# Token norms of a two-layer transformer kernel: root and reciprocal with the tokens on the partitions

## The reference

```python
def rms_norm(t, g):
    tf = t.astype(jnp.float32)
    y = tf * lax.rsqrt(jnp.mean(tf * tf, axis=-1, keepdims=True) + EPS)
    return y.astype(t.dtype) * g

def modulate_2(t, g, shift, scale):
    return rms_norm(t, g) * (1 + scale) + shift
```

## The kernel before

| norm | place | tokens | turn on TensorE behind the sums | first product |
|---|---|---|---|---|
| 1 | before feed-forward 1 | 256 | none | L318 |
| 2 | before the mixer | 256 | `after`, 32 records | L318 |
| 3 | before feed-forward 2 | 256 | none | L318 |
| 4 | before MLA | 512 | `late`, 32 records | L1758 |
| 5 | before PEER, layer 0 | 512 | `after`, 32 records | L318 |
| 6 | before the differential attention | 512 | `late`, 64 records | L1675 |
| 7 | before PEER, layer 1 | 256 | none | L318 |

## Time and profile before

### The profile page before, as it was taken

The page is one execution under the profiler, slowest core; times in us unless marked ns, Lnnn a source line. Parts: engine busy times, 40 slices in busy tenths (PEclk is TensorE's granted clock), DMA queues, the critical chain, the costliest instruction groups (busy, mean ns, idle before and its releaser), DMA issues.

```text
span 3421.4 us, 53779 instructions
## 1 busy us (share of the span) xinstructions
PE 3250.2 (95%) x20550; PEld 2969.2 (87%) x20550; DVE 2388.9 (70%) x3963; ACT 1430.3 (42%) x1692; POOL 1060.6 (31%) x670
## 2 busy tenths in 40 slices
PE   7999889998999999899989999999988999999998
PEld 5999689755877999898989999997778999988787
DVE  6877577685753689987749989986664965026665
ACT  5435244323533333365523333324334468434443
POOL 0110000010000477776754335540001976740000
PEclk9999799999999999999999999999999999999999
DMA  8884157451022377799999999983114669768885
GB/s 317 333 293 167 50 193 251 159 192 55 1 75 89 117 270 257 250 361 362 383 353 394 379 386 406 409 337 111 38 59 157 230 211 306 258 232 289 298 286 206
DMA packets 305190, 814.27 MB, mean 238 GB/s; under 512 B 21760, under 2 KB 188928, under 8 KB 253696
## 3 DMA queue, kind: packets, MB, share of 16 engines
q1 hardware_dynamic: 241856, 583.07, 47.7%
q0 software_dynamic: 58752, 213.94, 16.7%
q10 hardware_dynamic: 4416, 15.05, 1.1%
HBM read 722.84 MB, written 89.13 MB: 237 GB/s over the span
## 4 chain that ended last, share of the span: by engine, by line
PE 72%; DVE 10%; DMA 3%; ACT 2%; issue 1%; SPq 1%; POOL 0%; DVEq 0%; ACTq 0%; POOLq 0%
PE ps L2735 19%; PE ps L3048 14%; PE ps L3040 10%; PE ps L1675 5%; PE ps L861 3%; PE ps L2297 3%; PE ps L1420 2%; PE ps L2757 2%; PE ps L318 2%; PE ps L872 2%; PE ps L1403 2%; PE ps L2137 1%; DVE arena L2773 1%; DMA arena<-activations 1%; DVE arena L2517 1%
## 5 line engine op out<-in xcount | busy, mean ns | idle before, releaser
L2735 PE MATMUL ps<-xT_split,arena_split 128*128 128x384 f32 (+1 forms) x4096 | 915.6, 312 | 15.0 <-POOL arena_split L2708 8.3
L2708 POOL TENSOR_TENSOR arena_split<-ring,arena_split 128x1024 fp32r<-128x1024 f32 x256 | 631.9, 2479 | 932.6 <-ACT arena_split L2662 931.5
L2735 PEld LDWEIGHTS ps<-xT_split,arena_split 128*128 128x128 f32 x4096 | 697.0, 191 | 16.3 <-issue 13.6
L2735 PE MATMUL ps<-hT_split,arena_split 128*128 128x384 f32 (+1 forms) x2048 | 634.8, 310 | 0.0
L3048 PE MATMUL ps<-arena_split 128*128 128x384 f32 x3072 | 535.4, 335 | 13.3 <-DVE arena_split L3000 13.3
L3048 PEld LDWEIGHTS ps<-arena_split 128*128 128x128 f32 x3072 | 534.2, 188 | 14.5 <-issue 12.3
L285 DVE TENSOR_TENSOR arena_split<-ring,arena_split 128x2048 fp32r<-128x2048 f32 x128 | 292.9, 2292 | 246.8 <-ACT arena_split L279 245.9
L2973 ACT ACTIVATE arena_split<-ring 128x2048 fp32r<-128x2048 f32 x128 | 245.5, 1918 | 482.6 <-PE ps L3048 287.7
L279 ACT ACTIVATE arena_split<-ring 128x2048 fp32r<-128x2048 f32 x128 | 244.4, 1915 | 378.5 <-PE ps L861 133.3
L2735 PEld LDWEIGHTS ps<-hT_split,arena_split 128*128 128x128 f32 x2048 | 391.9, 191 | 0.0
L2997 DVE TENSOR_TENSOR arena_split<-ring,arena_split 128x2048 fp32r<-128x2048 f32 x128 | 293.1, 2290 | 102.6 <-ACT arena_split L2973 102.6
(11 more groups left out here) (319 smaller groups left out, 5117.7 us busy)
## 6 DMA issues: line engine op xcount, KB each, us to landing
ring<-in_weights SPq DMA_DIRECT2D x396, 1024.0 KB, 5.2
arena<-in_side_weights POOLq DMA_DIRECT2D x152, 512.0 KB, 5.6
gates<-arena SPq DMA_DIRECT2D x48, 512.0 KB, 11.6
arena<-gates SPq DMA_DIRECT2D x32, 768.0 KB, 12.5
arena<-activations SPq DMA_DIRECT2D x64, 384.0 KB, 10.6
activations<-arena SPq DMA_DIRECT2D x128, 128.0 KB, 3.0
gates<-arena SPq DMA_DIRECT2D x16, 1024.0 KB, 7.8
arena<-gates SPq DMA_DIRECT2D x64, 256.0 KB, 5.1
```

Source lines behind the costliest of these rows:

```text
L2708: pool.tensor_tensor(low, self.raw(f)[:, j, :], high.bitcast(F32), ALU.subtract)\
L2735: mm = pe.matmul(k.ps[:, j, 0:self.T], self.u[:, 2 * (f % 2) + j, a, t * P:(t + 1) * P], self.h[b][:, t, :], start=n == 0, stop=n == 3 * D ...
```

## The change

A class `TokenRoots` takes the place of the sums, root and reciprocal of `Norm`:

- `table` runs a root of one column on ScalarE ahead of the squares.
- `add` takes 128 tokens of a squared tile as the stationary operand and one column of ones as the moving one, so the sum lands with tokens on the partitions, one column for each 128 tokens.
- `roots` and `invert` work on 2 or 4 columns; `invert` then scales the identity by each column.
- `along_tokens` multiplies ones by each scaled identity, which writes the reciprocal of every token along the free axis on all partitions, into bank 5. The scaling of the tiles reads it there, in PSUM.
- TensorE's order is now: sums, turn `late`, `along_tokens`, turn `after`.

```diff
+class TokenRoots:
+    def __init__(self, k, T, bank):
+        self.k, self.T, self.n = k, T, T // P
+        self.bank = bank
+        self.root, self.inv = k.root[:, 0:self.n], k.root[:, 8:8 + self.n]
+        self.diag = k.rstd[:, 0:T].rearrange("p (q n) -> p q n", n=P)
+        self.rstd = k.ps[:, bank, 0:T]
...
+    def table(self, act):
+        act.wait_ge(self.k.ones_ready.sem, self.k.ones_ready.at(1))
+        act.activation(self.k.small[:, 400:401], self.k.eps[:, 0:1], ACT.Sqrt)
+
+    def add(self, pe, t, sq):
+        for q in range(self.n):
+            mm = pe.matmul(self.k.ps[:, 0, q:q + 1], sq[:, q * P:(q + 1) * P], self.k.ones[:, 0:1],
+                           start=t == 0 and q == 0, stop=t == DT - 1, skip_group_check=True)
+        if t == DT - 1:
+            mm.then_inc(self.sums.sem, 1)
+
+    def roots(self, act):
+        act.wait_ge(self.sums.sem, self.sums.at(1))
+        act.activation(self.root, self.k.ps[:, 0, 0:self.n], ACT.Sqrt, bias=self.k.eps[:, 0:1],
+                       scale=1.0 / D).then_inc(self.rooted.sem, 1)
+
+    def invert(self, dve):
+        dve.wait_ge(self.rooted.sem, self.rooted.at(1))
+        dve.reciprocal(self.inv, self.root).then_inc(self.inverse.sem, 1)
+        dve.wait_ge(self.inverse.sem, self.inverse.at(1))
+        for q in range(self.n):
+            dve.tensor_scalar(self.diag[:, q, :], self.k.ident, self.inv[:, q:q + 1], None, ALU.mult)\
+               .then_inc(self.placed.sem, 1)
+
+    def along_tokens(self, pe):
+        for q in range(self.n):
+            pe.wait_ge(self.placed.sem, self.placed.at(q + 1))
+            mm = pe.matmul(self.k.ps[:, self.bank, q * P:(q + 1) * P], self.k.ones[:], self.diag[:, q, :],
+                           start=True, stop=True)
+        mm.then_inc(self.spread.sem, 1)
+
+    def wait_spread(self, dve):
+        dve.wait_ge(self.spread.sem, self.spread.at(1))
...
     def scalar(self, act):
         k, w = self.k, slice(self.lo, self.hi)
+        self.roots.table(act)
         for t in range(DT):
...
-        mean_root(k, act, self.sums, self.hi - self.lo, D, self.root)
+        self.roots.roots(act)
...
             pe.wait_ge(self.squares.sem, self.squares.at(t + 1))
-            mm = pe.matmul(k.ps[:, 0, 0:self.hi - self.lo], k.ones[:], self.sq[:, t, w], start=t == 0, stop=t == DT - 1)
-        mm.then_inc(self.sums.sem, 1)
-        for turn in (self.late, self.after):
-            if turn:
-                turn.tensor(pe)
+            self.roots.add(pe, t, self.sq[:, t, w])
+        if self.late:
+            self.late.tensor(pe)
+        self.roots.along_tokens(pe)
+        if self.after:
+            self.after.tensor(pe)
...
-        dve.wait_ge(self.root.sem, self.root.at(1))
-        dve.reciprocal(k.rstd[:, 0:T], k.root[:, 0:T]).then_inc(self.inverse.sem, 1)
-        dve.wait_ge(self.inverse.sem, self.inverse.at(1))
+        self.roots.invert(dve)
         if self.late:
             self.late.vector(dve)
+        self.roots.wait_spread(dve)
...
                 dve.scalar_tensor_tensor(k.hT[:, t, lo:hi], k.xT[:, t, lo:hi], gain[:, t:t + 1],
-                                         k.rstd[:, lo - self.lo:hi - self.lo], ALU.mult, ALU.mult)\
+                                         self.roots.rstd[:, lo - self.lo:hi - self.lo], ALU.mult, ALU.mult)\
                    .then_inc(self.scaled.sem, 1)
```

More of the change, by code:

```diff
@@ L656, in mean_root @@
                    scale=1.0 / width).then_inc(root_ready.sem, 1)
+class TokenRoots:
[5 more added lines that the diff above has]
+        self.rstd = k.ps[:, bank, 0:T]
+        self.sums = k.count_of("norm_sums", 1)
+        self.rooted = k.count_of("norm_root", 1)
+        self.inverse = k.count_of("norm_inverse", 1)
+        self.placed = k.count_of("norm_diag", self.n)
+        self.spread = k.count_of("norm_spread", 1)
+    def table(self, act):
[26 more added lines that the diff above has]
+        dve.wait_ge(self.spread.sem, self.spread.at(1))
 class Norm(Stage):
@@ L673, in __init__ @@
         self.squares = k.count_of("norm_squares", DT)
-        self.sums = k.count_of("norm_sums", 1)
-        self.root = k.count_of("norm_root", 1)
-        self.inverse = k.count_of("norm_inverse", 1)
+        self.roots = TokenRoots(k, self.hi - self.lo, 5)
         self.scaled = k.count_of("norm_scaled", DT * len(parts))
```

## The result

The changed kernel takes 3438.4 us (median), the kernel before in the same series 3421.9. The ratio is 1.005, 95% interval [1.0039, 1.0062]: slower, by 16.5 us, where the forecast was +9.6; the time lies 0.6 us inside the upper end of the forecast's range. The profiled execution has a span of 3438.3 us and a time of its own of 3440.1, so 1.8 us lie around the span; the forecast added its sum to a span as if nothing did.

The account below looks back on a forecast made before the run. TensorE, busy 95% of the span, was taken as the bound, each norm costing a wait plus products at the lower clock. Shifts 1.2 + 1.8 - 0.2 + 3.1 + 0.4 + 3.8 - 0.5 = +9.6 on 3421.4 gave 3431.0 us, range 3412 to 3439.

Parts of the forecast that it names:

- Rival (a): Narrow sums: one-column products count as work for the clock, which stays up; sum -7.6, 3413.8 us; chance 0.27.
- Rival (d): Narrow sums: the clock falls, but a one-column record keeps 0.11 us; +0.6, 3422.0 us; chance 0.03.
- Rival (c): Root in seven norms: the early table does not last, each pays up to 1.28 us; 3440 us; chance 0.05.
- norms 1, 3, 4 and 5: Forecast shifts of the work that follows each norm: +1.2, -0.2, +3.1 and +0.4 us.
- TensorE wins back 1.5 where it waited for a split chunk (L977): Norm 2: of 3.3 us lost to the turn `after`, 1.5 regained at that wait, leaving +1.8 us.
- norms 2 and 6: Forecast shifts of the work that follows these norms: +1.8 and +3.8 us.
- a fall at 3.8 us and a rise 4.4 us behind the turn's start: Norm 6: clock drops 3.8 us into the narrow sums, returns 4.4 us into the turn `late`.
- 0.7 is won back at a split chunk: Norm 6, behind the first product: 0.7 us of the delay regained, leaving +3.8 us.
- my lower end of 2.3: Narrow sums: earliest clock fall assumed, 2.3 us after their start, from a one-column stretch.
- the middle of two rows, 3.8 us: Narrow sums: clock fall taken between 2.3 us (one-column stretch) and 5.3 us (L1764's stretch).
- Norm 7: Forecast -0.5 us: full clock in the sums, which end as it falls; the rest shrinks from 2.3 to 1.8.

Follow-up runs that it names:

- e1: The changed kernel with the sums moving 128 columns of ones instead of one; 3415.6 us, ratio 0.9987 against the kernel before.
- e8: The changed kernel run once more, nothing altered, for a second trace; ratio 1.0045 against the kernel before.
- e4: The changed kernel with the new form only in the norms of 512 tokens (4, 5, 6), the old form elsewhere; ratio 1.003 against the kernel before.
- e6: The changed kernel with the turn `after` put ahead of the spreading (`along_tokens`) again; ratio 1.0065 against the kernel before.

## Why the prediction was right and wrong

**Right: the mechanism and the sign.** Clock 1.00 at the start of the narrow sums and 0.50 later, in norms 4, 5 and 6, with 0.11 and then 0.21 us a record. Rival (a), that the clock stays, falls by norm 5's window above; what it said would follow is what e1 measured, where the clock did stay: -1.9 and -5.4 us for norms 4 and 5 there, -1.5 and -5.0 here. Rival (d), a load that keeps its pace, falls too: L682's records, as far apart with one column (0.11 us) as e1's with 128, double in distance when the clock falls. The Trainium skill (TensorE: Matmul & The Clock Gate, section LDWEIGHTS) gives a load's time as its columns over 1.2 GHz, with no word of the clock, which makes an estimate of 107 ns for 128 columns. At clock 1.00 the trace agrees, with 0.11 us a record; at 0.50 it does not, with 0.21. Rival (c) falls: the table load stands ahead of the squares and no other comes before the root.

**Right within 0.5 us: norms 1, 3, 4 and 5.** Norm 1's scaling starts at 47.19 (forecast 47.2), and the reason is the forecast one: the load at 35.14 pushes the low halves. They move by 1.1 us, not 1.5, and what follows them takes 0.4 us longer than forecast, two small misses that cancel. The timelines of ScalarE and VectorE in norm 1, the answer to the earlier trace rows:

```profile
35.14 1.28 ACT L677 ACT_TABLE_LOAD   x1 [0.72 <-issue]
36.44 0.20 ACT L677 ACTIVATE small<-eps 128x1 f32<-128x1 f32 x1
36.55 2.54 ACT L744 ACTIVATE hT<-xT 128x256 f32<-128x256 f32 x8
```

```profile
40.99 4.49 DVE L285 TENSOR_TENSOR arena_split<-ring,arena_split 128x2048 fp32r<-128x2048 f32 x2 [4.97 <-ACT arena_split L279]
45.40 0.15 DVE L696 RECIPROCAL root<-root 128x2 f32<-128x2 f32 x1
45.59 0.48 DVE L699 TENSOR_SCALAR rstd<-rows,root 128x128 f32<-128x128 f32 x2
47.19 0.87 DVE L800 SCALAR_TENSOR_TENSOR hT<-xT,coef,ps 128x256 f32<-128x256 f32 x2 [1.12 <-PE ps L706]
```

In norm 4 (TensorE's timeline, the answer to the earlier trace rows) the narrow sums take 10.4 us (forecast 10.1), the turn 5.3 (5.6), and the clock is back before the first product:

```profile
658.31 10.50 PE L682 MATMUL ps<-ones,arena 128*128 128x1 f32 x64 [0.75 <-ACT arena L744]
668.67 5.50 PE L630 MATMUL ps<-ones,hT 128*128 128x128 f32 x32
674.01 1.06 PE L706 MATMUL ps<-rstd,ones 128*128 128x128 f32 x8
676.74 1.55 PE L1812 MATMUL ps<-hT,ring 128*128 128x512 f32 x3 [1.67 <-ACT hT L758]
```

In norm 5 the shift is right partly by luck. The sums took 11.4 us (forecast 10.1), so that scaling starts 1.9 us later counted from the start of the sums (forecast 0.6); but the clock came back early in the turn, which took 4.4 us instead of the forecast 5.6.

Also right: reading the reciprocals from PSUM costs nothing. L800 has a mean of 475 ns; L746 had 481.

**Wrong: the size of two terms, norms 2 and 6, 5.8 of the 7.4 us that the sum was short.**

The step that failed in norm 2 is "TensorE wins back 1.5 where it waited for a split chunk (L977)". The first product came at 267.35, 3.6 us later counted from the shift before it (forecast 3.3), and all 3.6 stayed. That wait is no slack. ScalarE's high half of the next chunk goes into a buffer that the early products L318 release, so the later products release it later, and L977 (L1031 after) waits as long as before, 1.53 us against 1.54. The timelines of ScalarE, VectorE and TensorE after:

```profile
276.35 1.92 ACT L279 ACTIVATE arena_split<-ring 128x2048 fp32r<-128x2048 f32 x1 [7.74 <-PE ps L318]
```

```profile
278.29 2.29 DVE L285 TENSOR_TENSOR arena_split<-ring,arena_split 128x2048 fp32r<-128x2048 f32 x1 [8.13 <-ACT arena_split L279]
```

```profile
280.64 0.39 PE L1031 MATMUL ps<-arena_split 128*128 128x256 f32 x1 [1.53 <-DVE arena_split L285]
```

VectorE's low half started at 273.55 before, 4.7 us earlier, which is the whole delay at that point. The row was there to be read before the prediction, and I read only the first releaser. From the kernel before, VectorE's low half and what released ScalarE's high half ahead of it:

```profile
271.61 1.92 ACT L279 ACTIVATE arena_split<-ring 128x2048 fp32r<-128x2048 f32 x1 [4.16 <-PE ps L318]
```

```profile
273.55 2.29 DVE L285 TENSOR_TENSOR arena_split<-ring,arena_split 128x2048 fp32r<-128x2048 f32 x1 [4.54 <-ACT arena_split L279]
```

In norm 6 the failed steps are the time at the lower clock (a fall at 3.8 us and a rise 4.4 us behind the turn's start, so 10.7 us; measured 13.7) and "0.7 is won back at a split chunk". TensorE's timeline, the answer to the earlier trace rows:

```profile
2315.59 12.17 PE L682 MATMUL ps<-ones,arena 128*128 128x1 f32 x64 [1.70 <-ACT arena L744]
2327.62 7.25 PE L630 MATMUL ps<-ones,hT 128*128 128x128 f32 x48
2334.71 1.95 PE L630 MATMUL ps<-ones,arena 128*128 128x128 f32 x16
2336.50 1.06 PE L706 MATMUL ps<-rstd,ones 128*128 128x128 f32 x8
2340.17 0.73 PE L1729 MATMUL ps<-arena_split 128*128 128x512 f32 x2 [2.62 <-DVE hT_split L794]
...
2354.77 1.06 PE L1729 MATMUL ps<-arena_split 128*128 128x512 f32 x2 [1.80 <-DVE arena_split L285]
```

The clock fell 1.8 us into the sums, under my lower end of 2.3, and they took 12.0 us, 1.9 more than forecast. The turn's 8.9 us are as forecast (9.1). The two give what the scaling lost beyond the forecast (+6.2 counted from the sums' start, forecast +4.5). Here the products behind are paced by VectorE, whose scaling and low parts stand in front of the next low half: the wait for L285 was 0.7 us before and is 1.80 now, so that chunk starts 6.2 us later counted from the shift before the norm: what the first products had won by a higher clock is given back at this wait, and nothing of the 6.2 is won. Behind that wait the windows show the clock at 0.50 again:

```profile
2344.80:2354.90 10.10, 8.30 (x37) 6.54 (x37) 8.05 (x17) 6.55 (x9) 0.00 (x0) 1.00 0.01 2
2355.10:2358.30 3.20, 3.20 (x9) 2.41 (x8) 2.51 (x2) 0.30 (x1) 0.00 (x0) 0.50 0.75 228
```

That is the remaining 1.6 us, half of the 3.4 us that this stretch lasts. In e8's norm 6 the same wait is 1.75 us, no such fall follows, and the shift is +6.2.

**What sized the term.** For the fall I took the middle of two rows, 3.8 us. Over the 12 narrow sums of 512 tokens in four traces (changed kernel, e4, e6, e8) it fell after 1.4 to 4.0 us, 2.9 in the mean. The lower of my two rows was weak evidence in any case: in it the clock fell at 36.15, behind the one-column products and 0.3 us into the wide sums of norm 1. But the moment of the fall alone does not set the loss. Norm 6 in four executions, in us, the second and the last two columns counted from the start of the sums:

| run | clock falls | at 0.50 for | sums end | first product |
|---|---|---|---|---|
| changed kernel | 1.8 | 13.7 | 12.0 | 24.6 |
| e8 | 2.0 | 13.7 | 11.9 | 24.6 |
| e4 | 3.1 | 13.7 | 10.9 | 24.6 |
| e6 | 1.4 | 17.1 | 12.4 | 26.2 |

e4 has the fall nearest to my forecast, and still the whole 6.2 us over the 18.4 of the kernel before: its sums are shorter, but the clock comes back later in the turn, which takes longer. With the width alone changed back (e1), the same chain takes 18.1 us without the lower clock. The windows at the lower clock in e4 and e8:

```profile
2307.20:2320.70 13.50, 13.50 (x65) 13.50 (x65) 7.06 (x12) 5.75 (x6) 0.00 (x0) 0.50 0.41 154
2312.80:2326.40 13.60, 13.60 (x65) 13.60 (x65) 8.30 (x15) 6.66 (x8) 0.00 (x0) 0.50 0.36 139
```

Both hold 65 records, as the changed kernel's stretch does, each 0.10 us dearer than at the full clock. So what was mis-sized is how long the lower clock lasts over sums and turn together. What sets that length no run here shows. In norms 1 and 3 the lower clock begins within 1 us of the start of the sums and lasts longer than I counted (from 37.3 to 54.4, and from 443.5 to 460.6), but behind the first product it lasts as long as before (5.6 and 5.3 us against 5.6 and 5.5), and so it costs little.

**Norm 7** gave 0.0 and +1.3 instead of -0.5. The forecast had the sums end as the clock falls. It fell 4.2 us behind their start in the changed kernel, when they had ended, and 2.6 in e8, within them. Counted from the start of the sums, the first product comes 0.2 us earlier in the one and 0.6 later in the other, and the products behind it then run 3.5 and 4.5 us at the lower clock, where they ran 3.0 before.

## What to carry to other kernels

Here a product whose moving operand is one column was no cheaper than one of 128, with a load of 128 columns before each, and the clock fell in a run of them although TensorE looked fully busy; the same run with 128 columns kept it. No width between the two was tried in the sums. When a step puts TensorE into a chain that used to leave it free, look at what was running there in the shade. And don't count a wait as slack before the releaser of its releaser is known: a wait on a buffer that the delayed engine itself frees moves along with the delay.

## What had not been expected of the hardware

Widening the moving operand 128 times made the sums faster: 64 records in 7.3 us instead of 11.4. And the waits around a norm were worth more in clock than in time: norm 5 gains 5.0 us in e1, of which 2.3 are the earlier first product (12.8 us from the start of the sums instead of 15.1) and 2.7 the products at the full clock.
